# Normed rows in front of the router: written in natural order, read as weights at every eighth channel

## The reference

```python
def trunk_layer(x, mod, s0_f, s0_b, n_seg, p):
    ...
    x = x + gt1 * rms_norm(mix, p['post_mix_g'])
    h2 = rms_norm(x, p['pre_ffn_g']) * (1.0 + sc2) + sh2
    x = x + gt2 * rms_norm(routed_ffn(h2, p), p['post_ffn_g'])

def routed_ffn(h, p):
    logits = (tok @ p['router_w'] + p['router_b'])
    top_val, top_idx = lax.top_k(logits, TOP_K)          # 4 of 32 experts
    gate = jax.nn.softmax(top_val, axis=-1)
    ...
    def expert_block(args):
        xb = tok_pad[idx]                                 # gathered rows of h2
        gu = xb @ p['w_gu'][e] + p['b_gu'][e]             # 1024 -> 2048
        act = x_glu * jax.nn.sigmoid(1.702 * x_glu) * (x_lin + 1.0)
        out = act @ p['w_down'][e] + p['b_down'][e]       # 1024 -> 1024
        return out * g[:, None]
```

## Time and profile before

| what | value |
|---|---|
| three runs | 1242.78, 1245.08, 1247.40 us (median 1245.08) |
| profiled execution, own time | 1245.22 us |
| its span, first to last instruction | 1243.4 us |
| PE busy | 1163.2 us (94%) |
| PEld busy | 553.0 us (44%) |
| DVE busy | 410.4 us (33%) |
| ACT busy | 202.5 us (16%) |
| POOL busy | 97.8 us (8%) |
| moved by DMA | 456.37 MB |
| mean granted TensorE clock | 0.982 of 2.4 GHz |

### The profile page before, as it was taken

One profiled execution on the slowest core, in us unless ns is written; L12 is line 12 of the kernel. 1 busy time (PEld: TensorE's weight loads), 2 busy tenths in 40 slices (PEclk: granted clock), 3 DMA queues, 4 the chain that ended last, 5 costly groups with the idle time before them and its releaser, 6 DMA issues.

```text
span 1243.4 us, 15249 instructions
## 1 busy us (share of the span) xinstructions
PE 1163.2 (94%) x6030; PEld 553.0 (44%) x6030; DVE 410.4 (33%) x940; ACT 202.5 (16%) x447; POOL 97.8 (8%) x136
## 2 busy tenths in 40 slices
PE   5999999999999999999999898989999898989897
PEld 3886888874433333333343333333433333333332
DVE  0698778774412121212132121212122221212123
ACT  2312233333110101010111111110101111111102
POOL 1002664441000000000000000000000000000000
PEclk9999999999999999999999999999999999999999
DMA  9901453339999999999999999999999999999996
GB/s 372 386 15 49 178 219 136 136 102 378 427 433 429 429 428 431 430 431 434 432 433 427 433 427 435 428 425 429 425 435 430 431 430 430 432 430 433 423 425 245
DMA packets 36394, 456.37 MB, mean 367 GB/s; under 512 B 4832, under 2 KB 5360, under 8 KB 15368
## 3 DMA queue, kind: packets, MB, share of 16 engines
q1 hardware_dynamic: 34480, 451.82, 86.1%
q0 software_dynamic: 1568, 3.98, 1.0%
q10 hardware_dynamic: 312, 0.11, 0.0%
HBM read 454.56 MB, written 1.34 MB: 367 GB/s over the span
## 4 chain that ended last, share of the span: by engine, by line
PE 56%; DMA 40%; DVE 2%; issue 1%; ACT 1%; SPq 0%; ACTq 0%; DVEq 0%
DMA ring<-in_w_gu 39%; PE bank L541 25%; PE bank L578 5%; PE bank L660 4%; PE bank L772 2%; PE bank L762 2%; PE bank L869 2%; PE bank L503 1%; PE bank L771 1%; PE bank L493 1%; PE bank L670 1%; PE bank L655 1%; PE bank L711 1%; PE bank L601 1%; PE bank L528 1%
## 5 line engine op out<-in xcount | busy, mean ns | idle before, releaser
L541 PE MATMUL bank<-ring,front 128*64 128x512 f32 x2048 | 468.5, 613 | 39.6 <-DMA ring<-in_w_gu 39.6
L541 PEld LDWEIGHTS bank<-ring,front 128*64 128x64 f32 x2048 | 146.1, 140 | 359.8 <-issue 288.3
L1364 DVE TENSOR_SCALAR front<-bank 128x512 f32<-128x512 f32 x32 | 22.1, 692 | 516.6 <-PE bank L541 516.6
L578 PE MATMUL bank<-front 128*64 128x512 f32 x512 | 113.4, 595 | 8.1 <-ACT front L994 8.1
L578 PE MATMUL bank<-ring,front 128*64 128x512 f32 x512 | 113.4, 595 | 5.2 <-ACT front L994 5.2
L986 ACT ACTIVATE front<-front 128x512 f32<-128x512 f32 x32 | 20.2, 630 | 523.1 <-DVE front L1364 523.1
L1387 DVE COPY front<-bank 64x512 f32<-64x512 f32 x32 | 21.9, 683 | 165.3 <-PE bank L578 165.3
L578 PEld LDWEIGHTS bank<-front 128*64 128x64 f32 x512 | 35.3, 137 | 75.9 <-issue 64.0
L578 PEld LDWEIGHTS bank<-ring,front 128*64 128x64 f32 x512 | 36.5, 137 | 71.9 <-issue 71.4
L503 PE MATMUL bank<-front 128*128 128x512 f32 x136 | 62.9, 605 | 0.9 <-DVE front L1387 0.9
L1481 DVE SCALAR_TENSOR_TENSOR front<-front 128x286 f32<-128x286 f32 x120 | 58.8, 540 | 0.5
(11 more groups left out here) (259 smaller groups left out, 1011.9 us busy)
## 6 DMA issues: line engine op xcount, KB each, us to landing
ring<-in_w_gu SPq DMA_DIRECT2D x54, 4096.0 KB
ring<-in_w_down SPq DMA_DIRECT2D x32, 2048.0 KB, 19.2
front<-in_w_down SPq DMA_DIRECT2D x32, 2048.0 KB, 19.7
ring<-in_w_gu SPq DMA_DIRECT2D x18, 2048.0 KB
ring<-in_ada_w SPq DMA_DIRECT2D x24, 1024.0 KB, 11.1
ring<-in_w_in SPq DMA_DIRECT2D x5, 2048.0 KB, 19.8
ring<-in_w_out SPq DMA_DIRECT2D x1, 4096.0 KB, 13.5
ring<-in_w_gu SPq DMA_DIRECT2D x4, 1024.0 KB
```

Of the source, the lines that this page charges most:

```text
L541: last = pe.matmul(ps[r][64 * hf:64 * hf + 64, :], xT[:, k, S * q:S * q + S], wgu[:, k, r * F + hf * 512:r * F + hf * 512 + 512], start=Fa ...
L578: last = pe.matmul(ps[2][64 * c:64 * c + 64, :], actT[:, m, 64 * hf:64 * hf + 64], wdn[q][hf][:, m, c * 512:(c + 1) * 512], start=(k == 0) ...
```

## The change

L1695 writes h2 in natural order, with plain 128x512 operands; the view `h2_by_row` is now a view of the naturally ordered rows that picks, for chunk c, every eighth column. `turn_h2`, `gather_first` and `gather` load their weights through it: 128 columns at a stride of 32 bytes where they were neighbours. The numbers computed are the same, and no instruction is added, removed or moved to another place.

```diff
-        h2_by_row = view(r_L[:, 0:2048], "p (g k r) -> p g r k", g=G, k=KC)
+        h2_by_row = view(r_L[:, 0:2048], "p (g r k) -> p g k r", g=G, k=KC)
...
@@ gather
-                    last = pe.matmul(ps[4 + c // 4][:, (c % 4) * P:(c % 4 + 1) * P], h2[:, g, c * P:(c + 1) * P],
+                    last = pe.matmul(ps[4 + c // 4][:, (c % 4) * P:(c % 4 + 1) * P], h2_by_row[:, g, c],
                                      sel[:, g].rearrange("p q s -> p (q s)"), start=(g == 0), stop=(g == G - 1))
...
@@ turn_h2
                     last = pe.transpose(ps[4 + 2 * g + c // 4][:, (c % 4) * P:(c % 4 + 1) * P],
-                                        h2[:, g, c * P:(c + 1) * P], ident)
+                                        h2_by_row[:, g, c], ident)
...
@@ vector engine, last step of the norm in front of the router
-                    v.scalar_tensor_tensor(h2_by_row[:, g, n % 2 * 64:n % 2 * 64 + 64, :],
-                                           h2n[:, g, cols].rearrange("p (r k) -> p r k", k=KC), rs2[:, g:g + 1],
-                                           b2b[:, n, :].rearrange("p (r k) -> p r k", k=KC), ALU.mult, ALU.add).then_inc(s["h2"], 1)
+                    v.scalar_tensor_tensor(h2[:, g, cols], h2n[:, g, cols], rs2[:, g:g + 1], b2b[:, n, :], ALU.mult, ALU.add).then_inc(s["h2"], 1)
```

## The result

The changed kernel takes 1251.97 us (median of 6 runs, 1251.08 to 1252.93) against 1245.15 us before on the same chip: ratio 1.0052, 95% interval 1.0041 to 1.0064. It is 6.8 us slower, just past the bound of 0.5% (6.2 us), which the lower end of the interval doesn't reach. The profiled execution took 1251.08 us with a span of 1249.2, 5.8 above the span before. The forecast was 1246.9, in a range of 1242.8 to 1263.

A forecast was written before the change was run, and what follows sets the result against it. The DMA stream was taken to bound the kernel; 0 (DVE) + 0 (router) + 0 (14 gathers) + 2.5 (last gather) - 0.8 (clock) = +1.7 us on 1245.2 gave 1246.9 us, range 1242.8 to 1263.

The forecast's parts named there:

- The middle case: Gather's load spacing grows by 20 to 150 ns, hidden but for the tail: 1245 to 1249 us, chance 0.53.
- the PE-bound rival: Loop's gather above 160 ns more a load makes each pair longer than 58.4 us: 1263 to 1326 us, chance 0.20.
- The two signs by which the forecast would be wrong: In the changed profile, PE's waits on `w_gu` vanish and the stream's GB/s falls below 430.
- What bounds the kernel: One unbroken DMA stream, mostly expert weights, to about 1228 us; PE time added behind 1157.87 shows in full.
- DVE's four writes: L1695 falls from 1090 to about 750 ns each, 1.4 us of DVE saved, hidden by the stream: 0.
- Price of a strided load: Each gather weight load 85 ns longer, by DVE's scattered write; spacing 77 ns more, 2.5 us a gather.
- the upper end: The longer load no longer overlaps its matmul: spacing 184 ns more, 5.9 us a gather.
- Where the 2.5 us go: Loop gathers fit into 5.1 us of PE spare per pair; loads issued later into a non-empty queue: cost 0.
- Router path: In front of the loop, 40 strided loads add 3.1 us, less than the 4.9 us queued: cost 0.
- Tail: The last gather, at 1166.86, shows in full: +2.5 us.
- Clock: Up-projection at 1157.87 may escape the clock's fall after a shorter wait; even chance, half of 1.7 us counted: -0.8.
- the stride is free: Strided loads cost nothing; the only effect is DVE's 1.4 us, hidden: 1245.2 us, chance 0.25.

The follow-up runs named there:

- experiment 2: Changed kernel with only the loop's gather put back to neighbouring columns; natural writes and strided loads in front of the loop stay: 1245.82 us, ratio 1.0000.
- experiment 3: Changed kernel with the loop's gather strided only in the first 8 pairs, at neighbouring columns in the last 7: 1245.22 us, ratio 0.9995.
- experiment 9: Kernel before plus 18 unused matmuls on neighbouring columns behind each gather of the loop, no strided read: 1250.73 us, ratio 1.0050.
- experiment 10: Kernel before plus 9 unused matmuls on neighbouring columns behind each gather of the loop, no strided read: 1247.19 us, ratio 1.0020.
- experiment 6: Changed kernel with only the very last gather of the loop strided, the other fourteen at neighbouring columns: 1250.10 us, ratio 1.0040.
- AHEAD = 5: Changed kernel with SP's change of load order (w_gu ahead of w_down) moved from the ninth pair to the sixth: 1251.93 us, ratio 1.0065.
- experiment 5: Changed kernel with the loop's gather strided only in pairs 9 to 14, the other nine at neighbouring columns: 1251.46 us, ratio 1.0050.
- experiment 4: Changed kernel with the loop's gather strided only in the last 7 pairs, at neighbouring columns in the first 8: 1253.76 us, ratio 1.0064.

## Why the prediction was right or wrong

The time lies in the stated range, but not for the reason of the forecast. The middle case, 1245 to 1249 us, missed it, and +6.8 us is four times the forecast +1.7. The range holds 1251.97 only because it reached up to the PE-bound rival, so that much was luck. The two signs by which the forecast would be wrong both came in part: the waits on `w_gu` fell from 39.6 to 4.4 us, and four slices of the stream fell to 403 to 421 GB/s.

**What bounds the kernel: right.** The DMA stream does, and PE shows only behind its last wait and where it holds up the stream. I saw the first of these places, not the second.

**DVE's four writes: right,** 1090 to 749 ns, and no gain can be told in experiment 2.

**Price of a strided load: the mechanism was right, the term too small.** "The load becomes 189 ns and sets the spacing, 77 more than 112: 32 x 77 = 2.5 us a gather." Measured: the load's recorded time grew by 144 ns, not 85, and the spacing by 127, so 4.07 us. Doubling the 104 ns, as the prediction read the Trainium skill's rule ("SBUF — State Buffer", the passage on cachelines), would have given 3.1: nearer, still short. Load and matmul do still overlap; the upper end with its 5.9 us did not come.

**"Where the 2.5 us go ... into a queue that is not empty. Cost 0": the step that failed.** It holds for the steady loop (experiment 3: 4.07 us a pair cost nothing over 8 pairs). It doesn't at the change of SP's order, where the issue of the next reload hangs on PE just when the queue is nearly used up. By experiments 9 and 10 the cover there is above 1.7 us and below 3.75 a pair; for "nothing until the spare time is used up, at 160 ns more a load" it should have been 5.1. Close to the forecast's price the step held (experiment 10, 1.7 us a pair: +1.9 us in all, the tail's part); with 4.07 it cost 3.4 us in the profiled execution. The spare time, too, was taken from one stretch and used for all: from 816.72 to 1157.87 the weights arrive over 341.15 us, in which PE needs 6 x 53.28 = 319.7, so it has 3.6 us to spare a pair and not 5.1. At 4.07 that is used up even if the stream has no hole.

**Router path: right,** and experiment 2 shows no loss. The 32 loads of `gather_first` at 127 ns more are 4.1 us, within the 4.9 queued at least. The transposes, counted at 77 ns each in the forecast, take no longer: eight of them before, and in the changed kernel:

```profile
301.35 1.04 PE L882 MATMUL bank<-front 128*128 128x128 f32 x8
...
301.01 1.04 PE L882 MATMUL bank<-front 128*128 128x128 f32 x8
```

The reload was issued at 321.18 in place of 320.73, only 0.45 us later, while the granted clock stayed at 1.00 from 308 to 312 us, where it was 0.55 before. That DVE's shorter write, and with it PE's shorter idle time, is the cause is argued, not shown.

**Tail: right in kind.** Last gather in full (experiment 6), 4.07 for 2.5.

**Clock: half counted, whole got,** in the profiled pair, and the change need not have done it: experiment 2's profile has the same half at full clock too.

```profile
1157.50 7.09 PE L541 MATMUL bank<-ring,front 128*64 128x512 f32 x32 [0.91 <-DMA ring<-in_w_gu]
```

From its start to the end it takes 83.9 us (1157.50 to 1241.4) where the kernel before took 85.5. Measured against that, the change costs 7.4 us. The medians' 6.8 lie between.

**The sum:** 0 + 0 + 0 + 2.5 - 0.8 = 1.7 became 0 + 0 + 3.4 + 4.1 - 1.7 = 5.8 in the spans. The rival "the stride is free" fell. The PE-bound rival did not come about as put (58.4 us a pair was not reached). But it had the right sign, and in the last third, where the weights come at 56.9 us a pair, PE with 57.35 indeed hardly waits.

What stays open: how the 3.4 us of the changed kernel divide between late transfers and a late PE. PE's own sum makes 2.9 of them. The transfers are late by 3.5 us in experiment 9, 4.0 with AHEAD = 5 and 4.6 in experiment 5, where PE waits for them. Open too is what `AHEAD` = 5 or 11 does to the kernel before, and whether a gentler order of loads would free it.

## What to carry to other kernels

A slack per iteration, read in the steady state, is good for the steady state only. Where a hand-written order of transfers changes, look for the issue that waits on the engine you are about to slow, and ask how much is queued at that moment. For fp32 weights of TensorE a stride of two elements was free (196 against 192 ns for 128 columns), and one of four or more cost about one ns an element; so did a stride of eight for a moving operand. Put the scatter on an engine whose time is hidden.

## What the hardware showed that was not expected

The transposes' loads at the stride (L882) went from 141 ns, the time of neighbouring ones, to 191 ns, 50 for 128 columns, where the fp32 matmuls' loads grew by 144; and eight of them took 1.04 us in both kernels. A load at every 8th column (337 ns) was longer than at every 5th or 16th (314, 312). And the kernels of experiments 2, 4, 5 and 6, whose instructions are the same up to there, came to the same wait up to 4.7 us apart between profiled executions (816.4 to 821.1), so spans are best compared from a common wait on.
